# Opening of a two-layer encoder: warming products, the variance and the first modulation column in another order

## The reference, cut to what matters

```python
def _rmsnorm(x, g):
    xf = x.astype(jnp.float32)
    y = xf * lax.rsqrt(jnp.mean(xf * xf, axis=-1, keepdims=True) + EPS)
    return (y * g.astype(jnp.float32)).astype(x.dtype)

def _modulation(c, w_mod, b_mod):
    m = jax.nn.silu(c) @ w_mod + b_mod
    shift, scale, gate = jnp.split(m, 3, axis=-1)
    return shift[:, None, :], scale[:, None, :], gate[:, None, :]

def reference(x, c, norm_g, w_mod, b_mod, a_w_in, ...):
    for i in range(DEPTH):                       # DEPTH = 2
        shift, scale, gate = _modulation(c, w_mod[i], b_mod[i])
        h = _rmsnorm(x, norm_g[i]) * (1.0 + scale) + shift
        y = _short_conv_mixer(h, ...) if i == 0 else _spatial_gating_mixer(h, ...)
        x = x + gate * y
    return _rmsnorm(x, final_g)
```

## Time and profile before

| what | value |
|---|---|
| three runs, us | 821.09, 821.37, 823.55 (median 821.37) |
| the profiled execution, us | 824.04 |
| its span, first to last instruction, us | 821.8 |
| PE busy | 804.2 us, 98% of the span |
| PEld busy | 752.4 us, 92% |
| DVE busy | 645.6 us, 79% |
| ACT busy | 438.5 us, 53% |
| POOL busy | 50.7 us, 6% |
| DMA | 137.84 MB, mean 168 GB/s; in the opening slices 350 and 345 GB/s |

### The profile page before, as it was taken

The page is one execution under the profiler, slowest core; times in us unless marked ns, Lnnn a source line. Parts: engine busy times, 40 slices in busy tenths (PEclk is TensorE's granted clock), DMA queues, the critical chain, the costliest instruction groups (busy, mean ns, idle before and its releaser), DMA issues.

```text
span 821.8 us, 15171 instructions
## 1 busy us (share of the span) xinstructions
PE 804.2 (98%) x5590; PEld 752.4 (92%) x5590; DVE 645.6 (79%) x942; ACT 438.5 (53%) x616; POOL 50.7 (6%) x64
## 2 busy tenths in 40 slices
PE   6999999999999999999999999999999999999996
PEld 6778999999999999987889888899999999988896
DVE  4989999999999999898553786657888888896534
ACT  3576665656656566553222854445676777752220
POOL 1010000000000000000000000010000000000000
PEclk9999999999999999999999999999999999999999
DMA  9885475656666656577421262405554454487103
GB/s 350 345 206 154 154 198 170 195 172 186 179 179 179 186 171 198 169 280 304 161 91 52 78 234 98 129 29 150 154 153 128 134 147 144 137 303 261 52 1 103
DMA packets 39501, 137.84 MB, mean 168 GB/s; under 512 B 4272, under 2 KB 6448, under 8 KB 39472
## 3 DMA queue, kind: packets, MB, share of 16 engines
q1 hardware_dynamic: 32128, 111.16, 36.9%
q0 software_dynamic: 6912, 25.17, 16.3%
q10 hardware_dynamic: 432, 1.13, 0.4%
HBM read 108.09 MB, written 4.19 MB: 137 GB/s over the span
## 4 chain that ended last, share of the span: by engine, by line
PE 93%; DVE 4%; DMA 1%; issue 1%; ACT 1%; SPq 0%; DVEq 0%; ACTq 0%
PE pp L1122 11%; PE pp L1123 11%; PE pp L1124 11%; PE pp L987 8%; PE pp L988 8%; PE pp L989 8%; PE p_aux L1122 7%; PE p_aux L1124 7%; PE p_aux L1123 7%; PE pp L1258 4%; PE pp L1259 4%; PE pp L1260 4%; PE p_aux L1332 2%; DVE acc_s L1418 1%; PE pp L1077 1%; DMA raw_s<-in_stream 1%
## 5 line engine op out<-in xcount | busy, mean ns | idle before, releaser
L1122 PE MATMUL pp<-h_hi,wh 128*128 128x256 f32 x280 | 79.3, 283 | 0.0
L1124 PE MATMUL pp<-h_hi,wl 128*128 128x256 f32 x280 | 79.2, 283 | 0.0
L1123 PE MATMUL pp<-h_lo,wh 128*128 128x256 f32 x280 | 79.2, 283 | 0.0
L1623 DVE TENSOR_TENSOR wl<-wt,wh 128x1024 fp32r<-128x1024 f32 x56 | 66.5, 1217 | 0.2 <-ACT wh L660 0.2
L660 ACT ACTIVATE wh<-wt 128x1024 fp32r<-128x1024 f32 x56 | 58.9, 1054 | 13.6 <-DVE wt L1604 7.6
L571 ACT ACTIVATE w_hi<-raw 128x1024 fp32r<-128x1024 f32 x29 | 30.6, 1058 | 61.8 <-PE pp L989 29.0
L1122 PE MATMUL pp<-s_hi,wh 128*128 128x256 f32 x224 | 63.4, 283 | 0.0
L1123 PE MATMUL pp<-s_lo,wh 128*128 128x256 f32 x224 | 63.4, 283 | 0.0
L1124 PE MATMUL p_aux<-s_hi,wl 128*128 128x256 f32 x224 | 63.4, 283 | 0.0
L1124 PE MATMUL pp<-s_hi,wl 128*128 128x256 f32 x224 | 63.4, 283 | 0.0
L1123 PE MATMUL p_aux<-s_lo,wh 128*128 128x256 f32 x224 | 63.4, 283 | 0.0
(11 more groups left out here) (223 smaller groups left out, 2591.8 us busy)
## 6 DMA issues: line engine op xcount, KB each, us to landing
raw<-in_stream SPq DMA_DIRECT2D x144, 512.0 KB, 4.0
wl<-raw POOLq DMA_DIRECT2D x28, 512.0 KB, 4.5
raw_l<-in_stream SPq DMA_DIRECT2D x18, 512.0 KB, 5.5
raw_s<-in_stream SPq DMA_DIRECT2D x16, 512.0 KB, 13.3
wl_b<-raw POOLq DMA_DIRECT2D x16, 512.0 KB, 4.5
raw_m<-in_stream SPq DMA_DIRECT2D x14, 512.0 KB, 3.2
x_s<-in_xt SPq DMA_DIRECT2D x4, 512.0 KB, 6.0
w_lo_s<-raw POOLq DMA_DIRECT2D x4, 512.0 KB, 5.4
```

Of the source, the lines that this page charges most:

```text
L1122: pe.matmul(out, hi, hi_of(k), start=fresh and k == 0, stop=False, skip_group_check=not fresh)
L1123: pe.matmul(out, hi, lo_of(k), start=False, stop=False, skip_group_check=not fresh)
L1124: mm = pe.matmul(out, lo, hi_of(k), start=False, stop=k == 3, skip_group_check=not fresh)
L1623: dve.tensor_tensor(wl[par][:, part], wt[par][:, part], f32(wh[par][:, part]), ALU.subtract).then_inc(t_cut, 1)
```

## The change

Six edits, all in the opening:

1. PE's first keep_clock grows from 6 to 28 products and waits for the constants alone, no longer for the first square.
2. PE's start_columns(0) moves behind the broadcast of 1/rms.
3. keep_clock(3) is put ahead of the broadcast, and the keep_clock(2) that stood behind direct_columns(1, 0) moves ahead of the wait for `amp_ready`.
4. On DVE, the variance comes after one modulation tile (kt = 4) and no longer after two.
5. DVE's diagonals come ahead of tile kt = 7 and no longer behind it; between the variance and the diagonals stand now tiles 5 and 6, where 6 and 7 stood.
6. DVE scales tile 0 before it makes the first `amp`, and tile 1 after it; before, `amp` came first and then both. scale_tile is scale_pair's body for one tile.

```diff
--- before.py
+++ after.py
@@ -49,7 +49,7 @@
 SQ_STEPS = 1 + 6 + 2
 SQ_START = 7
 FREE = 2
-WARM = (6, 2)
+WARM = (28, 3, 2)
 WARM_END = 8
 LEAD = 0
 AHEAD = 3
@@ -1054,7 +1054,6 @@
 
 
             pe.wait_ge(consts, 3)
-            pe.wait_ge(sq_ready, 1)
             keep_clock(WARM[0])
             pe.wait_ge(wide_ready, 1)
             direct_columns(0, 0)
@@ -1063,11 +1062,12 @@
                 mm = pe.matmul(p_rstd[:, st:st + 1], ssum[:, P * st:P * (st + 1)], ones[:, 0:1], start=True, stop=True)
             mm.then_inc(stat_sum, 1)
             direct_columns(0, 1)
+            keep_clock(WARM[1])
+            broadcast(p_rstd[:, :], 2, ALL)
             start_columns(0)
-            broadcast(p_rstd[:, :], 2, ALL)
+            keep_clock(WARM[2])
             pe.wait_ge(amp_ready, 1)
             direct_columns(1, 0)
-            keep_clock(WARM[1])
             for kp in range(4):
                 w = (0, 1, 3, 4)[kp]
                 pe.wait_ge(hi_cut, CUT_ORDER.index(w) + 1)
@@ -1488,8 +1488,12 @@
             def scale_pair(kp, scale, where, layer=1):
 
                 for k in (2 * kp, 2 * kp + 1):
-                    dve.tensor_tensor(staged(layer, k, where), (x if layer else x_s)[:, k, where], scale,
-                                      ALU.mult).then_inc(h_scaled, 1)
+                    scale_tile(k, scale, where, layer)
+
+            def scale_tile(k, scale, where, layer):
+
+                dve.tensor_tensor(staged(layer, k, where), (x if layer else x_s)[:, k, where], scale,
+                                  ALU.mult).then_inc(h_scaled, 1)
 
             def cut_h_pair(done, kp, where):
                 for k in (2 * kp, 2 * kp + 1):
@@ -1511,15 +1515,16 @@
                     dve.wait_ge(sq_added, k - 1)
                 dve.tensor_tensor(ssum[:, :], ssum[:, :] if k > 1 else x_squared(0), x_squared(k),
                                   ALU.add).then_inc(sq_added, 1)
-            start_tiles(0, 4, 5)
+            start_tiles(0, 4)
             dve.wait_ge(stat_sum, 1)
             rsqrt(1, p_rstd[:, 0:NCH], 1.0 / D, NCH)
-            start_tiles(0, 6, 7)
+            start_tiles(0, 5, 6)
             dve.wait_ge(power_ready, 1)
             for st in range(2, 4):
                 ins = dve.tensor_scalar(work[:, 0, P * st:P * (st + 1)], ident[:, :], rstd[:, st:st + 1], None,
                                         ALU.mult)
             ins.then_inc(diag_ready, 1)
+            start_tiles(0, 7)
 
             def start_amp(kp):
                 dve.wait_ge(acc_used, kp + 1)
@@ -1535,9 +1540,10 @@
                 dve.tensor_tensor(amp[:, k:k + 2], amp[:, k:k + 2], cols[:, C_NORM + k:C_NORM + k + 2],
                                   ALU.mult).then_inc(amp_ready, 1)
 
+            dve.wait_ge(rstd_bc, 1)
+            scale_tile(0, p_rstd[:, :], ALL, 0)
             start_amp(0)
-            dve.wait_ge(rstd_bc, 1)
-            scale_pair(0, p_rstd[:, :], ALL, 0)
+            scale_tile(1, p_rstd[:, :], ALL, 0)
             cut_lo_start(0)
             start_tiles(1, 2, 3)
             cut_h_tile(0, 0, ALL)
```

## The result

The changed kernel is slower: **823.9 us** in the median of 22 runs (821.88 to 828.17), against 821.4 us for the kernel before (22 runs, 820.73 to 825.96). The ratio is 1.0024, with a 95% interval from 1.0014 to 1.0034. I had forecast 820.5.

A forecast was written before the change was run, and what follows sets the result against it. PE was taken to bound the kernel (93% of the span), its opening at half clock speed. The opening's 3.7 us less 0.15 for weight 5 gave 824.04 - 3.55 = 820.5 us, range 817.6 to 822.2.

The forecast's parts named there:

- The opening: From warming to h_lo of tile 0: an early clock and the new order make h_hi 3.75 and h_lo 3.7 us earlier.
- x: Time in us from the start of PE's warming products until its clock rises; taken as 4 to 6, at price 0.
- The baseline: Profile lies 2.67 us above the median; the median was read as an execution whose clock rose earlier, near 14 us.
- rival D: Opening: products with ones don't bring PE's clock up, as 12 had not; some 826 us, chance 0.06.
- Weight 5: Its load lands at 37.3, wanted by ACT's cut at 35.7; h_hi of tile 4 late by 0.15 us.
- about 1 us is left: Margin between the landing of weight 5's low part, 2 us earlier instead of 3.7, and PE's need for it.
- rival C: Part of the gain lost: warming products overrun by up to 1.6 us or weight 5 lands later; 821.5 to 823, chance 0.12.
- An opening that ends earlier moves all that follows by as much: Whole kernel after the opening: 93% of the span hangs on PE, so the opening's 3.7 us would carry through.
- the times would lie closer together: Sign to look for: runs of the changed kernel spread less than those before, as the clock's rise no longer varies.

The follow-up runs named there:

- the second profile of before: The kernel before, unchanged, profiled in a second execution of 821.15 us; its direct columns ran at full speed from the first on.
- the run with the order alone: The changed kernel with its first warming back at six products behind the first square, keeping the new order of edits: ratio to before 0.9995 (0.9974 to 1.0016).
- The run with wide products: The changed kernel with its 28 warming products of 128 columns as 7 of 512 columns, 84 PE instructions fewer: 820.97 us median, ratio 0.9983.
- the pair with equal openings: The changed kernel, unchanged, and the same with 7 warming products of 512 columns for 28 of 128, on one chip: 823.58 and 820.97 us.
- the padded run: The kernel before with 100 empty PE semaphore increments ahead of PE's first wait, to shift its code: 830.98 us, ratio 1.0103.

## Why the prediction was wrong, point by point

- **The opening: right.** Warming from 1.7; rise at 5.3 to 7.2 us by the pace of the records in the five profiles with 28 products, x = 3.7 to 5.5 where 4 to 6 was taken, no cost; variance at 13.59 (forecast 13.85), broadcast 16.18 (16.4), h_hi 18.58 (18.9), h_lo 21.38 (21.7).
- **The baseline: right, with the wrong moment.** The median execution has most of the gain already. The reason given, an earlier rise, is shown by the second profile of before; the rise at 14 us was one of several that occur (13.7 in the run with the order alone). That second profile also takes back the support for rival D: the same 12 records, which "did not" raise the clock in the first profile, had a risen clock right behind them here.
- **Weight 5: half right.** ACT's cut at 37.22 (forecast 37.3), h_hi of tile 4 at 39.13 (39.35). The step "about 1 us is left" failed: it took the low part's latency of 5.0 as fixed. Weight 7's load is released by DVE and is issued 3.9 us earlier (40.15 against 44.05), while the low part is issued 2.2 us earlier; so the load now starts 0.6 us behind the low part, where it had started 2.3 behind (7.5 us; 4.8 when weight 7 is held back). PE waited 1.27 us, and the column sum came at 48.56, not 47.9. This is in kind what rival C named. The kernel before does the same in its second profile (7.5 us, PE waits 1.27), so against such an execution this costs nothing.
- **"An opening that ends earlier moves all that follows by as much": this is the step that failed.** It took a bound of 93% PE as proof that no later wait depends on anything but PE. The wait at 372 hangs on DMA; it stood in the profile of before already, as 0.87 us of idle at 373.70 with no releaser named, and was taken for nothing. And no term of the sum priced what 25 more products do other than take PE time: 100 more instructions, which move the code fetches. Measured against the profile with an early clock: 1.6 us more in that wait, and up to 1.4 for the clock that falls behind it. The run with wide products is the kernel whose time I had worked out: 820.97 against 820.5.
- **The rivals.** The slower rival, that products with ones don't raise the clock, did not happen. The slower result came by a mechanism that I had not listed. My forecast that the times would lie closer together failed for the same cause (821.88 to 828.17), and comes true when it is removed: 820.52 to 823.62 with the wide products, and 0.41 us in all with ScalarE's loads moved too.
- **Open.** That the fetch delays the slot is shown by the pair with equal openings and by the latencies: 9.1 to 9.3 in the five profiles with the fetch behind the first slot's landing and ACT's loads beside it, 9.8 to 10.8 in the four with the fetch ahead of it; in the padded run it starts only 0.7 us ahead of the landing, and the latency is 9.1. The fetch follows the length of the code in all 14 profiles: it comes 12.4 to 12.9 us behind the issue with none added, 12.1 with 4 instructions, 10.9 to 11.2 with 12 or 16, and 7.7 to 8.4 with 88 or 100, so not in proportion. Why the delay is up to 1.7 us, more than the packet's own 1.0, isn't settled. That the two waits are the whole loss is shown for an execution without a fall: the second profile of the changed kernel (823.17 us, idle 2.53) is 0.4 us behind the second of before (821.15) at 49 us, 2.0 behind it after the wait of 372, and 2.0 at the end.

## What to carry to other kernels

Filling PE's idle time isn't free just because PE is idle: each product is four instructions here, and as code is fetched while the kernel runs, it moves every fetch behind it. Where warming work is wanted, use few wide products instead of many narrow ones. Before reckoning that an earlier start moves the end by as much, look in the trace for every later place where PE waits for a chain that ends in DMA, even where it idles for less than 1 us; and where two executions of one kernel differ, take a second profile before choosing the baseline.

## What the runs showed of the hardware that was not expected

- A fetch of PE's code, one packet of 16 KB, holds a DMA engine for 0.9 to 2.1 us; the 512 KB transfer beside it landed up to 1.7 us later.
- The clock fell behind an idle of 2.57 us in one execution and did not behind one of 2.53 in another; it fell once behind 1.64, and not behind 1.80 elsewhere; behind the waits of 1.52 or less it fell in no profile. A fall lasted 3.4 us here, and 6.8 us once (the first edit alone, behind an idle of 2.00).
- An accumulating DMA of 512 KB that GpSimd issues took 4.8 us alone. With one load of 512 KB issued 2.0 to 2.3 us behind it, it took 5.0 to 5.3; 1.2 us behind it, 5.6; 0.4 to 0.8 us behind it, 7.2 to 8.2.
- A semaphore increment on PE that nobody waits for took 0.15 us.
